# Forgetting and stick-breaking attention: the head's values as stationary operand, outputs with features in rows, and the order of work at the ends of the stages

## The reference, cut to what matters

```python
# 8 forgetting heads and 8 stick-breaking heads of 64 features
fox:   p = softmax(q.k/sqrt(d) + c[t] - c[s], s <= t);            o = p @ v
stick: a = sigmoid(z) * prod_{s<j<t}(1 - sigmoid(z[t,j])), s < t; o = a @ v
mixed = concat([rmsnorm(fox_o, fox_out_g), rmsnorm(sb_o, sb_out_g)])   # over 512 features each
x = x + mixed @ w_out
x = x + softmax(q_m.k_m/16) @ v_m @ w_mo         # memory: 4 heads, 256 keys
...
x = x + mla(...) @ b_w_o_2                       # 8 heads of 128 (+64 rotary) features
```

## Time and profile before

| | |
|---|---|
| three runs, median (lowest to highest) | 2018.45 us (2017.95 to 2018.85) |
| the profiled execution: its own time | 2017.77 us |
| the profiled execution: span from first to last instruction | 2016.0 us |
| PE busy in it | 1994.7 us, 9471 matmuls |
| DVE, ACT, POOL busy | 1143.4, 756.2, 230.0 us |

### The profile page before, as it was taken

One profiled execution on the slowest core, in us unless ns is written; L12 is line 12 of the kernel. 1 busy time (PEld: TensorE's weight loads), 2 busy tenths in 40 slices (PEclk: granted clock), 3 DMA queues, 4 the chain that ended last, 5 costly groups with the idle time before them and its releaser, 6 DMA issues.

```text
span 2016.0 us, 23200 instructions
## 1 busy us (share of the span) xinstructions
PE 1994.7 (99%) x9471; PEld 1652.0 (82%) x9471; DVE 1143.4 (57%) x1619; ACT 756.2 (38%) x1199; POOL 230.0 (11%) x173
## 2 busy tenths in 40 slices
PE   9999999999999999999999999999999999999998
PEld 7888988888888888888888888888877778888887
DVE  5544677467765566737577444443587574333333
ACT  5353454335333334523324233223543353332224
POOL 1000230000000000000000232221211011222221
PEclk9999999999999999999999999999999999999999
DMA  5322212213232232323222323223232013223221
GB/s 172 105 84 63 89 59 84 84 41 105 85 105 91 98 104 88 122 84 104 84 84 89 105 84 105 94 95 105 73 91 93 22 42 105 90 98 105 95 94 63
DMA packets 140218, 180.52 MB, mean 90 GB/s; under 512 B 9680, under 2 KB 100944, under 8 KB 140112
## 3 DMA queue, kind: packets, MB, share of 16 engines
q1 hardware_dynamic: 138224, 177.52, 27.0%
q10 hardware_dynamic: 1632, 1.51, 0.3%
q0 software_dynamic: 256, 0.02, 0.0%
HBM read 176.91 MB, written 2.10 MB: 89 GB/s over the span
## 4 chain that ended last, share of the span: by engine, by line
PE 94%; DVE 5%; ACT 1%; issue 0%; POOL 0%; ACTq 0%; POOLq 0%
PE bank L498 26%; PE bank L500 25%; PE bank L499 25%; PE bank L660 5%; PE bank L541 2%; PE bank L543 2%; PE bank L542 2%; PE bank L652 1%; DVE w_lo L1109 1%; PE bank L740 1%; PE bank L736 1%; PE bank L946 1%; DVE arena L1148 1%; DVE resid L1171 0%; PE bank L666 0%
## 5 line engine op out<-in xcount | busy, mean ns | idle before, releaser
L498 PE MATMUL bank<-h_hi,w_hi 128*128 128x512 f32 x1384 | 545.5, 394 | 2.1 <-DVE w_lo L1109 2.1
L500 PE MATMUL bank<-h_hi,w_lo 128*128 128x512 f32 x1384 | 539.6, 390 | 0.0
L499 PE MATMUL bank<-h_lo,w_hi 128*128 128x512 f32 x1384 | 539.4, 390 | 0.0
L1877 ACT ACTIVATE w_hi<-raw 128x1024 fp32r<-128x1024 f32 (+2 forms) x335 | 331.1, 1030 | 493.4 <-PE bank L500 440.5
L498 PE MATMUL bank<-g_hi,w_hi 128*128 128x512 f32 (+1 forms) x972 | 377.1, 388 | 2.7 <-DVE w_lo L1109 1.5
L500 PE MATMUL bank<-g_hi,w_lo 128*128 128x512 f32 (+1 forms) x972 | 371.8, 383 | 0.0
L499 PE MATMUL bank<-g_lo,w_hi 128*128 128x512 f32 (+1 forms) x972 | 371.5, 382 | 0.0
L468 POOL TENSOR_TENSOR w_lo<-raw,w_hi 128x1024 fp32r<-128x1024 f32 (+1 forms) x75 | 181.5, 2420 | 1508.3 <-ACT w_hi L1877 1508.3
L1109 DVE TENSOR_TENSOR w_lo<-raw,w_hi 128x1024 fp32r<-128x1024 f32 (+2 forms) x258 | 307.4, 1215 | 61.4 <-ACT w_hi L1877 60.6
L1171 DVE TENSOR_TENSOR resid<-bank,resid 128x512 f32<-128x512 f32 x287 | 194.3, 687 | 228.4 <-PE bank L500 227.9
L498 PEld LDWEIGHTS bank<-h_hi,w_hi 128*128 128x128 f32 x1384 | 260.3, 188 | 58.2 <-issue 2.8
(11 more groups left out here) (241 smaller groups left out, 1745.1 us busy)
## 6 DMA issues: line engine op xcount, KB each, us to landing
raw<-w SPq DMA_DIRECT2D x64, 1024.0 KB, 5.2
raw<-w_up SPq DMA_DIRECT2D x22, 1024.0 KB, 5.1
raw<-a_w_in SPq DMA_DIRECT2D x16, 1024.0 KB, 5.2
raw<-w_in SPq DMA_DIRECT2D x11, 1024.0 KB, 5.2
raw<-w_down SPq DMA_DIRECT2D x11, 1024.0 KB, 5.1
raw<-w_mkv SPq DMA_DIRECT2D x8, 1024.0 KB, 5.5
raw<-a_w_out SPq DMA_DIRECT2D x8, 1024.0 KB, 5.0
raw<-w_out SPq DMA_DIRECT2D x4, 1024.0 KB, 5.0
```

Of the source, the lines that this page charges most:

```text
L498: nc.tensor.matmul(dst, a_hi, b_hi, start=(k == 0), stop=False)
L499: nc.tensor.matmul(dst, a_hi, b_lo, start=False, stop=False)
L500: last = nc.tensor.matmul(dst, a_lo, b_hi, start=False, stop=(k == n - 1))
L1877: A(hi, src, ACT.Copy).then_inc(w_hi_done, 1)
```

## The change

It does these things.

- **Values.** For fox and sb the head's 64 value columns become the stationary operand and the transposed probabilities (128 columns) the moving one; heads of odd number write partitions 64 to 127. The output bank has features in rows (`features_of`).
- **Fox probabilities are divided on DVE** before they are transposed, as in the other kinds; PE's transposes of fox wait for that (`p_ready`). The division per group goes.
- **No turning.** `turn_mixed` and its 32 transposes go, and with them `normed`, `high_of_mixed` and `take_mixed`. ACT squares each group (now without a sum), GpSimd adds the four tiles of squares in two additions (`sum_of_group`), PE sums over features with four one-column matmuls (`mix_sums`), ACT takes the root, DVE puts it on a diagonal (`row_of_mixed`), PE spreads it over the rows (`spread`), DVE scales four tiles with gain and row (`scale_mixed`), ACT and DVE make the halves.
- **Ends.** Fox: `mix_sums` after the second query tile, `spread` one chunk later. Sb: `mix_sums` after piece 2 and `spread` after piece 5 of `of_fox(1, ...)`; `back_tile(7)` moves behind the four low halves.
- **Lag 3** for memory and MLA, with a third probability buffer; the fillers start one step later. Memory's first scores no longer wait for all query tiles (`late`). In memory and MLA the low halves of a group now come ahead of the step's `back_tile`, and memory's weight pieces move.
- **Start.** The first two k tiles of x and of the weights come in loads of 256 KB each, in turn; `keep_busy(14)` becomes `keep_busy(10)`; the two `spread` matmuls move from behind `first_part` into its second pair of tiles, after k = 5.

```diff
-        LAG = {"fox": 3, "sb": 3, "mem": 2, "mla": 2}
+        LAG = 3
+        late_prob = [at(16384, S), at(16896, S), at(18944, S)]
...
-            for q in range(4):
+            for k in range(2):
+                sp.dma_start(x_stage[:, :, P * k:P * k + P], x_cols[:, :, P * k:P * k + P]).then_inc(x_first[k], 16)
+                sp.dma_start(quarter_view(raw, 0)[:, k:k + 1, :], first_rows[:, k:k + 1, 0:512]).then_inc(w_first[k], 16)
+            for q in range(1, 4):
...
+            def sum_of_group(g, total):
+                pool.wait_ge(group_squared, g + 1)
+                G.tensor_tensor(pair_sums, squared[:, 0:256], squared[:, 256:512], ALU.add).then_inc(group_summed, 1)
+                pool.wait_ge(group_summed, 2 * g + 1)
+                G.tensor_tensor(total, pair_sums[:, 0:P], pair_sums[:, P:256], ALU.add).then_inc(group_summed, 1)
...
             for n, (h, i) in enumerate(BLOCKS):
+                if n % HEADS == 6 and n > HEADS:
+                    g = n // HEADS - 1
+                    sum_of_group(4 + g, squares_sb[:, P * g:P * g + P])
...
-                        if kind == "fox":
-                            pe.wait_ge(s_taken, u + 1)
-                        else:
-                            pe.wait_ge(p_ready, u + 1 - len(BLOCKS))
+                        pe.wait_ge(p_ready, u + 1)
...
-            def head_values(v):
-                return lambda h, i, pt: several([(o_bank[:, HD * h:HD * h + HD], pt[:, P * k:P * k + P],
-                                                  v[:, k, HD * h:HD * h + HD], k == 0, k == i) for k in range(i + 1)])
+            def features_of(v):
+                return lambda h, i, pt: several([(o_bank[HD * (h % 2):HD * (h % 2) + HD, P * (h // 2):P * (h // 2) + P],
+                                                  v[:, k, HD * h:HD * h + HD], pt[:, P * k:P * k + P],
+                                                  k == 0, k == i) for k in range(i + 1)])
+            def mix_sums(acc, n, summed):
+                pe.wait_ge(group_summed, summed)
+                for t in range(TT):
+                    last = nc.tensor.matmul(col_bank[:, t:t + 1], acc[:, P * t:P * t + P], ones[:, 0:1], start=True, stop=True)
+                last.then_inc(mix_full, 1)
...
-            keep_busy(14)
+            keep_busy(10)
...
-            pe.wait_ge(x_copied, KT)
-            spread(1, stat_bank[:], diag_x)
-            spread(2, col_bank[:, 0:NMEM], diag_mem)
+                    if pair[0] == 2 and k == 5:
+                        pe.wait_ge(x_copied, KT)
+                        spread(1, stat_bank[:], diag_x)
+                        spread(2, col_bank[:, 0:NMEM], diag_mem)
...
-            attention("fox", BLOCKS, fox_scores, head_values(fox_v), beside_fox, v_tiles=4)
+            attention("fox", BLOCKS, fox_scores, features_of(fox_v), beside_fox, v_tiles=4)
             by_feature(first=1)
-            for c in range(3):
+            mix_sums(squares_fox, 0, 8)
+            by_feature()
+            spread(3, stat_bank[:], diag_fox)
+            for c in range(2):
                 by_feature()
...
             for piece in range(8):
                 of_fox(1, piece)
-            pe.wait_ge(t_made, 3)
-            for n in range(4):
-                turn_mixed(n)
+                if piece == 2:
+                    mix_sums(squares_sb, 0, 16)
+                elif piece == 5:
+                    spread(4, stat_bank[:], diag_sb)
...
             attention("mem", MEM_UNITS, mem_scores, mem_values,
-                      lambda s: back((s - 8) // 4, [s % 4 * 2, s % 4 * 2 + 1]) if s >= 8 else None)
+                      lambda s: back((s - 9) // 4, [(s - 9) % 4 * 2, (s - 9) % 4 * 2 + 1]) if s >= 9 else None,
+                      late=lambda s: max(0, 6 - 2 * (s // TT)))
...
-            attention("sb", BLOCKS, mixed_group("sb"), beside_sb)
-            normed()
+            attention("sb", BLOCKS, mixed_group, beside_sb)
             split_low()
-            for n in range(4, 8):
-                back_tile(n)
+            back_tile(4)
+            row_of_mixed(diag_sb)
+            back_tile(5)
+            back_tile(6)
+            scale_mixed(4, "sb_out_g")
             for n in range(4):
-                take_mixed(g_hi, g_lo, "sb_out_g", n)
+                low_of_mixed(g_lo, g_hi, n, g_ready)
+                g_n.n += 1
+            back_tile(7)
...
             def beside_mla(s):
-                if s >= 13:
-                    back_tile((s - 13) % 8)
-                if s >= 11 and s % 8 == 3:
+                if s >= 12 and s % 8 == 4:
                     lows_of_group(s // 8 - 1)
+                if s >= 14:
+                    back_tile((s - 14) % 8)
```

More of the change, by code:

```diff
@@ L118, in weight_stream @@
     out += tokens("w_in", 2) + mkv(0, 1, 2, 3) + tokens("w_in", 5) + w_in(3) + w_in(4)
-    out += mkv(4) + [("tiles", 2)] + mkv(5) + [("tiles", 2)] + mkv(6, 7) + down("w_out", 0) + [("tiles", 4)] + down("w_out", 1)
+    out += mkv(4) + mkv(5) + mkv(6, 7) + down("w_out", 0) + down("w_out", 1)
     out += [columns("w_mq", COLS * c) for c in range(4)] + [rows("w_mo", c) for c in range(4)]
@@ L619, in attention @@
                 v_end = tile.n
-                lag = LAG[kind]
+                lag = LAG
                 for s in range(n + lag + 1):
@@ L870, in _ @@
                         full(last)
+            g_n.n += 4
             chunk.n += 1
@@ L1205, in attention @@
             def attention(kind, units, out_group, between):
-                n, per, lag = len(units), GROUP[kind], LAG[kind]
+                n, per, lag = len(units), GROUP[kind], LAG
                 first = unit.n
@@ L1389, in normed, with scale_mixed, low_of_mixed @@
                 settle()
-                for t in range(TT):
-                    ins = V.tensor_scalar(mixed[:, t, :], mixed[:, t, :], mix_rs[:, t:t + 1], None, ALU.mult)
-                ins.then_inc(t_made, 1)
-                made.n += 1
-            def take_mixed(hi, lo, name, n):
-                dve.wait_ge(hi_done, hi_n.n + 1)
-                hi_n.n += 1
-                take(lambda b: V.scalar_tensor_tensor(lo[:, n, :], b[:], gain(name, n), hi[:, n, :].bitcast(F32),
-                                                      ALU.mult, ALU.subtract))
+                put_on_diagonal(diagonal, mix_rs)
+            def scale_mixed(n_spread, name):
+                dve.wait_ge(spread_full, n_spread)
+                for n in range(4):
+                    V.scalar_tensor_tensor(by_feature_sb[:, n, :], by_feature_sb[:, n, :], gain(name, n), stat_bank[:],
+                                           ALU.mult, ALU.mult).then_inc(t_made, 1)
+                    made.n += 1
+            def low_of_mixed(lo, hi, n, ready):
+                low_half(lo[:, n, :], hi[:, n, :], by_feature_sb[:, n, :], None, ready)
             def beside_fox(s):
@@ L2019, in _ @@
                 if n == 4:
-                    for q in range(4):
+                    for q in range(2):
+                        act.wait_ge(x_first[q], 16)
+                    for q in range(3):
                         act.wait_ge(x_loaded[q], 16)
@@ L2063, in mixed_root @@
             def mixed_root(n):
-                act.wait_ge(act_own, n)
-                A(mix_rs, mix_ss, ACT.Sqrt, scale=1.0 / 512, bias=eps_t).then_inc(act_out, 1)
+                act.wait_ge(mix_full, n)
+                A(mix_rs, col_bank[:, 0:TT], ACT.Sqrt, scale=1.0 / 512, bias=eps_t).then_inc(act_out, 1)
                 acts.n += 1
-            def high_of_mixed(hi, name, n):
-                act.wait_ge(tile_full, tile.n + 1)
-                A(hi[:, n, :], tile_bank[tile.n % 4][:], ACT.Copy, scale=gain(name, n)).then_inc(hi_done, 1)
-                hi_n.n += 1
-                tile.n += 1
             split_high()
             attention("fox", BLOCKS, squares_of_group(0, FOX_PIECES))
-            mixed_root(2 + 4)
             tile.n += KT + TT
-            for _ in range(3):
+            for n in range(3):
                 split_high()
+                if n == 0:
+                    mixed_root(1)
             tile.n += 4 + 4
-            made.n += 1
+            made.n += 4
+            act.wait_ge(t_made, made.n)
             def beside_sb(s):
@@ L2095, in _ @@
             tile.n += 4
+            mixed_root(2)
             for n in range(4):
-                high_of_mixed(g_hi, "sb_out_g", n)
+                made.n += 1
+                act.wait_ge(t_made, made.n)
+                high_half(g_hi[:, n, :], by_feature_sb[:, n, :])
             split_high()
```

140 lines of the change are left out of this document (67 added, 73 removed).

## The result

The changed kernel takes 2032.86 us (median of 4 runs: 2036.62, 2033.69, 2031.91 and 2032.03), beside 2018.65 us for the kernel before on the same chip. The ratio is 1.0075, with a 95% interval of 1.0061 to 1.0089. The forecast was 2011.4, a gain of 7; what came is a loss of 14.2, so the sign was wrong too. The profiled execution is the slowest of the four: 2036.62 us, with a span of 2034.9.

What follows compares the result with a forecast made beforehand. PE was taken as the bound, busy 1994.7 of 2016.0 us. Terms -2.7 + 2.0 - 0.1 + 1.0 - 4.3 - 0.9 - 1.3 - 0.7 = -7.0 gave 2011.4 us; range 2007.5 to 2015.5.

Steps and rivals of the forecast that it cites:

- the term of the values: Fox and sb value products with 64 stationary and 128 moving columns: +2.0 us, bounds 0 and +3.2.
- The third rival: Weight loads of the 320 value records no longer hidden, 0.08 us more each: 25 us, 2036; chance 5%.
- my own sign: Value records 0.13 us or more apart would show the forecast wrong; 0.11 or less would show it right.
- The +1.4: The values' term if, by the Trainium skill, a weight load lasts as long as its columns, so half here.
- Start and norms: First loads, filler and first norms' spread: -2.7 us, with PE next waiting about 1.9 us for DVE's copy.
- my bound of -1.1: Start and norms gain only this if the clock falls again behind the new wait for the copy.
- Turning, sums and spread: Fox transposes removed -3.5 us, one-column sums added +1.8, two spreads +1.6: together -0.1.
- Fox on DVE: Fox reciprocals and divisions added on DVE: 0 us, up to +3 if uncovered.
- The end of stick-breaking: PE waits 0.9 then 0.5 us at the stage's end, less the old 0.35: +1.0, between 0 and 3.
- Lag 3: Memory and MLA: the eight waits on DVE's division mostly go, -4.3 us, bounds -2.5 and -5.4.
- memory's start: Memory's first scores no longer wait for the last query tile: -0.9 us, 0 to -0.95.
- both ends: Waits for `w_lo` at memory's end and the group's low halves at MLA's end go: -1.3 and -0.7 us.

Runs made afterwards that it cites:

- full width: Changed kernel with 128 value columns stationary instead of 64: 2015.73 us with heads overwriting each other, 2017.10 us computing the whole reference.
- late parts: Kernel before with only lag 3 in memory and MLA, later fillers, memory's earlier scores, low halves ahead of back tiles and moved weight pieces: 2011.80 us.
- one side: Changed kernel with odd heads writing partitions 0 to 63 as even ones do, the stationary operand still 64 wide: 2032.50 us.

## Why the prediction was wrong

**The step that failed is the term of the values**, +2.0 with bounds of 0 and +3.2. Measured alone it was +20.9. I took eight value records of one shape and eight of the other, each from the first record to the transposes behind it, and multiplied a difference of 0.05 by 64. By the rows it is 0.89 - 0.83 = 0.06, which would have made the bound +3.8. For operands of one size that was right: full width costs 0.05 a unit. What I did not price is the border between two shapes. I wrote that no row shows a stationary operand 64 wide, and then bounded it by rows that all have one width from score to transpose. An operation that the trace doesn't show should have had a bound of a whole exposed load at each border: 0.19 twice a unit is 24 us, and the 18 us that the two changes cost lie inside it.

**The third rival** had the price (2036) and the word, loads no longer hidden, but the wrong place. It put 0.08 on each of 320 records and was to be recognised by records 0.13 apart. They are 0.11 apart, so by my own sign (0.13 or more) the forecast would have stood. A price by record and a price by border differ in where one looks: the distance inside the run, or from the record ahead of it to its first and from its last to the record behind. Its 5% was far too little for something that no row could exclude.

The Trainium skill ("TensorE: Matmul & The Clock Gate", LDWEIGHTS) gives a weight load a time in proportion to its columns. The trace agrees in part: the loads of 64 columns last 132 to 138 ns and those of 128 last 0.19 us, so they are shorter, but not by half. The +1.4 that the prediction drew from it would have missed as well.

The Trainium skill ("TensorE: Matmul & The Clock Gate", The mechanism) says in one line that a load overlaps a running product only where the row groups differ, and in another that a load into a background weight buffer is pulled ahead too. This trace disagrees with the first alone: the transposes' load, of 128 rows, starts at 142.43 above, while value records of 128 rows have PE until 142.54. What stopped such loads was a change to or from a size of 64 in rows or columns.

**Start and norms**, -2.7: part right, and too large: with the first product in time it gained 1.2 to 2.0. The `w_lo` wait at 39 us went, and the wait for the copy came back at 2.07 us (1.9 forecast). The small loads gained 0.1 us by the median of their first products (9.45 against 9.55), instead of 0.45. The clock, which I had hoped to get back, fell in the profiled execution behind that wait, as my bound of -1.1 had it: 9 records in 3.41 us at 0.50, its level of 1.2 GHz, then full speed.

```profile
57.78:61.20 3.41, 3.41 (x9) 2.63 (x9) 3.33 (x5) 2.15 (x3) 1.19 (x3) 0.50 0.94 303
61.20:64.00 2.80, 2.80 (x13) 2.29 (x13) 2.77 (x4) 0.12 (x1) 2.79 (x6) 1.00 0.05 7
```

In other executions the same wait left the clock at 1.00. With the first product in time, the first fox score came 1.2 to 2.0 us earlier than before (88.88 and 88.12 against 90.08).

**Turning, sums and spread:** the stretch from the last fox values to the first sb score grew by 2.04 us; half of the added 3.4 was forecast for it, 1.7. **Fox on DVE**, 0: right, no transpose of fox waited for the division. **The stick-breaking stage** had a wait that I had not listed, 1.03 us at 259.26 for DVE's product (L1246). In steps 4 and 8 DVE now makes two low halves from SBUF and sat idle 2.05 us ahead of them for ACT's high half, with the scan queued behind:

```profile
254.02 0.29 DVE L1246 TENSOR_TENSOR arena<-arena 128x128 f32<-128x128 f32 x1
256.37 1.39 DVE L1149 TENSOR_TENSOR h_lo<-arena,h_hi 128x512 fp32r<-128x512 f32 x2 [2.05 <-ACT h_hi L1912]
257.68 0.86 DVE L1311 TENSOR_SCALAR arena<-bank,rstd_col 128x256 f32<-128x256 f32 x2
258.47 0.41 DVE L1243 TENSOR_TENSOR_SCAN arena<-arena 128x128 f32<-128x128 f32 x1
```

**The end of stick-breaking**, +1.0: measured +0.95 with 0.69 us of idle time at 340.31, where 0.9 was forecast for the first low half. GpSimd's two additions took 0.73 and 0.46 us (0.7 and 0.4 forecast). **Lag 3**, -4.3: -3.74 in MLA and -0.16 in memory; **memory's start**, -0.9: -0.94; **both ends**, -1.3 and -0.7: -1.49 and -0.59. Measured together without the rest: -6.8 for -7.2.

The sum with the measured terms, in us: 2018.65 - 6.8 (late parts) + 20.9 (values) + 0.95 (end of stick-breaking) + 2.04 (fox sums and spread) - 1.8 (16 fox transposes at 0.11) + 1.0 (the new wait) and -1.2 to -2.0 (start) gives 2032.9 to 2033.7. The median is 2032.86. The terms come from medians and from single profiled executions, so an agreement this close is partly luck.

## What to carry to other kernels

Count changes of the stationary operand's size class, not only products. Turning operands around so that a head's 64 features are stationary, or dropping a score from 65 rows to 64, cost 0.28 us and 0.36 to 0.39 us each time a full-size product stood on both sides, and nothing between equals; pad to a full width, or put such products together. When an operation is new to a trace, price its two borders with an exposed load before pricing its middle. And check that the products are worth it even then: here the full width was still 8 us behind the old values. A change in many parts should be measured in parts: here 9.8 us of gain lay under 21 of loss.

## What the runs showed of the hardware that was not expected

- Weight loads run under the product ahead of them between the sizes 128 x 128, 65 x 128 and 128 x 96 (rows x columns), but not across a change to or from 128 x 64 or 64 x 128: 0.14 to 0.19 us for each such change (0.28 and 0.36 to 0.39 for two).
- The loading side's idle time on the values' line, put down to "issue", grew from 14.6 us before to 34.7 after, 17.7 with 96 columns. The answers on L660 of before, L682 of after and L682 of the kernel with 96 columns:

```profile
issue: 14.6, 61
```

```profile
issue: 34.7, 84
```

```profile
issue: 17.7, 76
```

- Which partitions of PSUM a 64-wide product writes, 0 to 63 or 64 to 127 in turn, made no difference (2032.50 against 2032.86 us).
- The same wait of 2.1 us near 55 us was followed by a stretch at 1.2 GHz in some executions and not in others (granted clock from 54 to 62 us 0.79 with one side, 1.00 with full width). It may be a part of the spread of 1 to 2 us between runs of one kernel; no run was made to show that.
